# Five edits at the start of a two-block transformer kernel: input squares folded, taps re-spread, one projection from native to split products

## The reference

```python
h = rmsnorm(x, norm_mix_g[0])
u = h @ w_pw1 + b_pw1                 # conformer_conv, 1024 -> 2048
a, gate = split(u); u = a * sigmoid(gate)
u = conv1d_depthwise(u, 31 taps) + b_dw
u = silu(layernorm(u, ln_g, ln_b))
x = x + u @ w_pw2 + b_pw2
h = rmsnorm(x, norm_mem_g[l]); mem_n = rmsnorm(mem, norm_memsrc_g[l])
k = mem_n @ w_k; v = mem_n @ w_v      # for layer l = 0 and l = 1
...                                   # attention, feed forward, the second block
```

## Time and profile before

| | us |
|---|---|
| runs, median (lowest to highest) | 1439.92 (1438.95 to 1442.92) |
| span of the profiled execution | 1437.8 |
| TensorE busy | 1411.5 (98%) |
| VectorE busy | 1111.5 (77%) |
| ScalarE busy | 690.4 (48%) |

### The profile page before, as it was taken

One profiled execution on the slowest core, in us unless ns is written; L12 is line 12 of the kernel. 1 busy time (PEld: TensorE's weight loads), 2 busy tenths in 40 slices (PEclk: granted clock), 3 DMA queues, 4 the chain that ended last, 5 costly groups with the idle time before them and its releaser, 6 DMA issues.

```text
span 1437.8 us, 21872 instructions
## 1 busy us (share of the span) xinstructions
PE 1411.5 (98%) x8580; PEld 1243.6 (86%) x8580; DVE 1111.5 (77%) x1660; ACT 690.4 (48%) x899; POOL 33.1 (2%) x21
## 2 busy tenths in 40 slices
PE   7999999999999999999999999999999999999997
PEld 6878998888889888888888988888988889888887
DVE  3799876698767887758887779997578678798664
ACT  2221664455434654645563355553454447555442
POOL 0000000000000000000000000000024100000000
PEclk9999999999999999999999999999999999999999
DMA  7444663355686456525558747757553436475451
GB/s 265 144 167 153 251 214 123 118 186 208 236 292 207 169 188 219 183 94 182 191 204 279 268 179 273 272 188 260 203 204 135 169 103 226 159 273 205 135 179 66
DMA packets 60150, 279.31 MB, mean 194 GB/s; under 512 B 6590, under 2 KB 8063, under 8 KB 35232
## 3 DMA queue, kind: packets, MB, share of 16 engines
q1 hardware_dynamic: 56248, 270.69, 53.7%
q10 hardware_dynamic: 3816, 7.45, 1.5%
HBM read 273.89 MB, written 4.19 MB: 193 GB/s over the span
## 4 chain that ended last, share of the span: by engine, by line
PE 84%; DVE 8%; DMA 5%; ACT 1%; issue 1%; DVEq 0%; SPq 0%; ACTq 0%
PE acc L477 34%; PE acc L479 17%; PE acc L498 10%; DMA ada_w<-in_ada 5%; PE acc L536 3%; PE acc L538 3%; PE acc L537 3%; DVE wsplit L1753 2%; PE acc L636 2%; PE stat L721 2%; DVE ada_w L2142 2%; PE acc L640 1%; PE turned L741 1%; PE stat L833 1%; PE score L1054 1%
## 5 line engine op out<-in xcount | busy, mean ns | idle before, releaser
L477 PE MATMUL acc<-hA,wsplit 128*128 128x512 f32 x1664 | 589.9, 399 | 4.4 <-DVE tsum L1767 1.7
L1176 ACT ACTIVATE wsplit<-raw 128x2048 fp32r<-128x2048 f32 (+3 forms) x214 | 381.2, 1783 | 195.3 <-PE acc L479 145.1
L1753 DVE TENSOR_TENSOR wsplit<-raw,wsplit 128x2048 fp32r<-128x2048 f32 (+3 forms) x214 | 455.1, 2130 | 16.4 <-ACT wsplit L1176 16.4
L479 PE MATMUL acc<-hA,wsplit 128*128 128x256 f32 x1664 | 463.9, 279 | 0.0
L477 PEld LDWEIGHTS acc<-hA,wsplit 128*128 128x128 f32 x1664 | 312.3, 188 | 81.6 <-issue 4.1
L479 PEld LDWEIGHTS acc<-hA,wsplit 128*128 128x128 f32 x1664 | 313.4, 188 | 0.4
L477 PE MATMUL acc<-hid,wsplit 128*128 128x512 f32 x648 | 224.9, 390 | 0.0
L479 PE MATMUL acc<-hid,wsplit 128*128 128x256 f32 x648 | 182.7, 282 | 0.0
L1186 ACT ACTIVATE lowp<-acc 128x512 f32<-128x512 f32 (+1 forms) x118 | 69.0, 585 | 202.8 <-PE acc L479 174.9
L477 PEld LDWEIGHTS acc<-hid,wsplit 128*128 128x128 f32 x648 | 121.6, 188 | 25.6
L479 PEld LDWEIGHTS acc<-hid,wsplit 128*128 128x128 f32 x648 | 122.5, 189 | 0.0
(11 more groups left out here) (315 smaller groups left out, 2051.6 us busy)
## 6 DMA issues: line engine op xcount, KB each, us to landing
raw<-in_gu SPq DMA_DIRECT2D x44, 1024.0 KB, 4.9
ada_w<-in_ada SPq DMA_DIRECT2D x144, 256.0 KB, 4.8
raw<-in_up SPq DMA_DIRECT2D x32, 1024.0 KB, 4.9
raw<-in_down SPq DMA_DIRECT2D x32, 1024.0 KB, 5.0
raw<-in_dn SPq DMA_DIRECT2D x32, 704.0 KB, 4.1
raw<-in_pw SPq DMA_DIRECT2D x12, 1024.0 KB, 8.1
raw<-in_memk SPq DMA_DIRECT2D x8, 1024.0 KB, 4.8
raw<-in_memv SPq DMA_DIRECT2D x8, 1024.0 KB, 5.3
```

The costliest lines, as they stand in the source:

```text
L477: nc.tensor.matmul(dst.rearrange("p (s t) -> p s t", s=2), w, h, start=start, stop=False, skip_group_check=True)
L479: return nc.tensor.matmul(dst[:, 0:T], lo_w, h[:, 0, :], start=False, stop=stop, skip_group_check=True)
L1176: nc.scalar.activation(wsplit[:, slot, 0, 0:elems_of(n)], raw[:, slot, 0:elems_of(n)], ACT.Copy).then_inc(S("w_hi"), 1)
L1753: V.tensor_tensor(wsplit[:, slot, 1, 0:e], raw[:, slot, 0:e], wsplit[:, slot, 0, 0:e].bitcast(F32), ALU.subtract).then_inc(S("w_lo"), 1)
```

## The change

1. **Input squares folded.** ScalarE writes the squares of x's four pairs to four places (`aux`, `tsum`); VectorE adds them with three additions (semaphore input_folded); TensorE needs 2 matmuls for the sum instead of 8, and issues them inside pw1's chunk 0, ahead of its sixth tile (`inside={(0, 5): input_sums}`), so that pw1 is first in its list. The load of `ones` moves behind that of the first weight chunk.
2. **Taps re-spread.** Each `expand` issues 2 taps before its product instead of 11, and then `BESIDE_PW1[c]` taps behind it: 97 in all during pw1 instead of 77.
3. **memk1 becomes a split stage** (`split_keys`, three matmuls for each tile into one bank). ScalarE's four `split_hi` stand in memv0's copies and behind them; VectorE's four `mem_lo` and three of the four `split_lo` come before the last taps.
4. **`ln_mean`** moves from behind memk1's chunk 2 to its tile 3.
5. **VectorE's later splits** all move back by a place: memv1's by one each, pw2's chunk 1 from between two `ln_lo` to behind the last one.

```diff
-NATIVE = ["pw1", "memk0", "memv0", "memk1"]
+NATIVE = ["pw1", "memk0", "memv0"]
+BESIDE_PW1 = [13, 12, 12, 16, 16, 2, 12, 0]
...
+            def split_keys():
+                st = STAGE["memk1"]
+                for c in range(st.chunks):
+                    weights_ready(st, c)
+                    pe.wait_ge(S("memory_kept"), 2 * (KT // 2) + c - 1)
+                    for kt in range(KT):
+                        if c == 0:
+                            pe.wait_ge(S("mem_lo"), kt // 2 + 1)
+                        if (c, kt) == (2, 3):
+                            ln_mean()
+                        for j in range(2):
+                            at = kt * 2 * P + j * P
+                            mm = whole_tile(acc[:, c % 2, j, 0:T], wsplit[:, c, 0, at:at + P], wsplit[:, c, 1, at:at + P],
+                                            tile_of(hA)(kt), kt == 0, kt == KT - 1)
+                    mm.then_inc(S("chunk_done"), 1)
...
-            pe.wait_ge(S("ones_loaded"), 16)
-            norm_sums("mix0")
+            def input_sums():
+                pe.wait_ge(S("ones_loaded"), 16)
+                pe.wait_ge(S("input_folded"), 3)
+                for j in range(2):
+                    mm = nc.tensor.matmul(stat[:, 0, :], ones[:], aux[:, 0, j, :], start=j == 0, stop=j == 1)
+                mm.then_inc(S("norm_stat"), 1)
...
-            native("memk1", mem_h[1], {kt: (S("mem_h"), KT + kt + 1) for kt in range(KT)},
-                   after=lambda c: ln_mean() if c == 2 else None)
+            split_keys()
             split_values()
...
+            nc.scalar.preload_act_table_set("natural_log_exp_and_others")
+            wait("x_loaded", 16)
+            for p in range(PAIRS):
+                nc.scalar.activation((aux if p < 2 else tsum)[:, p % 2, :, :], x[:, 2 * p:2 * p + 2, :],
+                                     ACT.Square).then_inc(S("norm_sq"), 1)
             wait("cols_loaded", 16)
...
+            def keys_ahead(c):
+                if c > 0:
+                    split_hi(STAGE["memk1"], c - 1, c - 1)
+                    return
+                wait("skew_stored", 16 * G_HEADS)
+                for p in range(PAIRS):
+                    wait("mem_h", KT + 2 * p + 2)
+                    nc.scalar.activation(hA[:, 2 * p:2 * p + 2, 0:T], mem_h[1][:, 2 * p:2 * p + 2, :],
+                                         ACT.Copy).then_inc(S("mem_hi"), 1)
+            memory_out("memv0", lambda c: mv0[:, :, c * T:(c + 1) * T], keys_ahead)
+            split_hi(STAGE["memk1"], 3, 3)
...
-                conv_taps(11, c)
+                conv_taps(2, c)
                 wait("pw1_sig", c + 1)
...
+                conv_taps(BESIDE_PW1[c], c + 1)
...
-            conv_taps(KT * TAPS, KT)
+            conv_taps(100, KT)
+            for p in range(PAIRS):
+                wait("mem_hi", p + 1)
+                V.tensor_tensor(hA[:, 2 * p:2 * p + 2, T:2 * T], mem_h[1][:, 2 * p:2 * p + 2, :],
+                                hA[:, 2 * p:2 * p + 2, 0:T].bitcast(F32), ALU.subtract).then_inc(S("mem_lo"), 1)
+            for c in range(3):
+                split_lo(STAGE["memk1"], c, c)
+                conv_taps(13 if c < 2 else KT * TAPS, KT)
...
             ln_fold(0, tsum[:, 0, :, :], tsum[:, 1, :, :], LN_MEAN)
-            for p in range(PAIRS):
-                wait("mem_hi", p + 1)
...
-            split_lo(STAGE["memv1"], 0, 0)
+            split_lo(STAGE["memk1"], 3, 3)
             wait("ln_stat", 1)
...
-            split_lo(STAGE["memv1"], 3, 3)
+            split_lo(STAGE["memv1"], 2, 2)
             ln_product(0)
             ln_product(1)
             ln_lo(0)
-            split_lo(STAGE["pw2"], 0, 0)
+            split_lo(STAGE["memv1"], 3, 3)
             ln_product(2)
             ln_lo(1)
-            split_lo(STAGE["pw2"], 1, 1)
+            split_lo(STAGE["pw2"], 0, 0)
             ln_product(3)
             ln_lo(2)
             ln_lo(3)
-            split_lo(STAGE["pw2"], 2, 2)
-            split_lo(STAGE["pw2"], 3, 3)
+            for c in range(1, STAGE["pw2"].chunks):
+                split_lo(STAGE["pw2"], c, c)
```

More of the change, by code:

```diff
@@ L175, in stat_count @@
 def stat_count(q):
-    return sum(2 if n in FOLDED else PAIRS for n, _ in NORMS[:q])
+    return sum(1 if n == "mix0" else 2 if n in FOLDED else PAIRS for n, _ in NORMS[:q])
 LN_TABLE = 3
+BESIDE_PW1 = [13, 12, 12, 16, 16, 2, 12, 0]
 LN_MEAN, LN_SQUARES = 3, 6
@@ L404, in _ @@
             sp.dma_start(cols[:], dram["cols"]).then_inc(S("cols_loaded"), 16)
-            sp.dma_start(ones[:], dram["ones"]).then_inc(S("ones_loaded"), 16)
             def load(st, c, known):
@@ L418, in _ @@
                 load(PLAN[0], c, c)
-                if c == 1:
+                if c == 0:
+                    sp.dma_start(ones[:], dram["ones"]).then_inc(S("ones_loaded"), 16)
+                elif c == 1:
                     for tensor, name in ((taps, "taps"), (ident, "ident"), (onehot, "onehot"), (relT, "relT"),
@@ L480, in block_cols, with native @@
                                         skip_group_check=True)
-            def native(name, h, ready=None, after=None):
+            def native(name, h, ready=None, after=None, inside={}):
                 st = STAGE[name]
@@ L490, in native @@
                     for kt in range(KT):
+                        if (c, kt) in inside:
+                            inside[c, kt]()
                         if c == 0 and ready and kt in ready:
@@ L873, in behind_pw1 @@
                     norm_sums("mem", [2 * c - 6, 2 * c - 5])
-            native("pw1", pw1_h, {2 * p: (S("pw1_h"), p + 1) for p in range(PAIRS)}, after=behind_pw1)
+            native("pw1", pw1_h, {2 * p: (S("pw1_h"), p + 1) for p in range(PAIRS)}, after=behind_pw1,
+                   inside={(0, 5): input_sums})
             def relative_biases(c):
@@ L1445, in log_sigmoid @@
                 nc.scalar.activation(za_, zl_, ACT.Ln, bias=1.0).then_inc(S(sem + "_ln"), 1)
+            nc.scalar.preload_act_table_set("natural_log_exp_and_others")
[3 more added lines that the diff above has]
+                                     ACT.Square).then_inc(S("norm_sq"), 1)
             wait("cols_loaded", 16)
-            log_table("mix0")
-            norm_squares("mix0", x, lambda p: [("x_loaded", 16)])
+            nc.scalar.activation(rstd[:, 0:1], col("rms_eps"), ACT.Ln).then_inc(S("log_table"), 1)
             norm_root("mix0")
@@ L1555, in _ @@
             beside = {
-                (0, 0): lambda: value_hi(0),
-                (0, 1): lambda: (ln_table(), value_hi(1)),
+                (0, 0): lambda: (ln_table(), value_hi(0)),
+                (0, 1): lambda: value_hi(1),
                 (0, 2): lambda: (ln_squares(range(PAIRS)), value_hi(2)),
@@ L1560, in _ @@
                 (1, 0): lambda: (ln_silu(0), ln_silu(1), ln_hi(0)),
-                (1, 1): lambda: (pw2_hi(0), ln_silu(2), ln_hi(1)),
-                (1, 2): lambda: (pw2_hi(1), ln_silu(3)),
+                (1, 1): lambda: (ln_silu(2), ln_hi(1), pw2_hi(0)),
+                (1, 2): lambda: (ln_silu(3), pw2_hi(1)),
                 (1, 3): lambda: (ln_hi(2), ln_hi(3), pw2_hi(2), pw2_hi(3)),
@@ L1565, in _ @@
             memory_out("memk0", lambda c: mk0[:, 2 * c:2 * c + 2, :], copy_biases)
-            memory_out("memv0", lambda c: mv0[:, :, c * T:(c + 1) * T])
-            wait("skew_stored", 16 * G_HEADS)
-            for p in range(PAIRS):
-                nc.scalar.activation(hA[:, 2 * p:2 * p + 2, 0:T], mem_h[1][:, 2 * p:2 * p + 2, :],
-                                     ACT.Copy).then_inc(S("mem_hi"), 1)
+            def keys_ahead(c):
[9 more added lines that the diff above has]
+            split_hi(STAGE["memk1"], 3, 3)
             memory_out("memk1", spill_at(0), spill_out(0))
@@ L2153, in _ @@
                 last.then_inc(S("pw1_h"), 1)
+            for i, (into, part) in enumerate(((aux[:, 0, :, :], aux[:, 1, :, :]), (tsum[:, 0, :, :], tsum[:, 1, :, :]),
+                                              (aux[:, 0, :, :], tsum[:, 0, :, :]))):
+                wait("norm_sq", 2 * i + 2 if i < 2 else PAIRS)
+                if i == 2:
+                    wait("input_folded", 2)
+                V.tensor_tensor(into, into, part, ALU.add).then_inc(S("input_folded"), 1)
             norm_scale("mix0")
@@ L2218, in _ @@
             ln_fold(0, tsum[:, 0, :, :], tsum[:, 1, :, :], LN_MEAN)
-            for p in range(PAIRS):
-                wait("mem_hi", p + 1)
-                V.tensor_tensor(hA[:, 2 * p:2 * p + 2, T:2 * T], mem_h[1][:, 2 * p:2 * p + 2, :],
-                                hA[:, 2 * p:2 * p + 2, 0:T].bitcast(F32), ALU.subtract).then_inc(S("mem_lo"), 1)
-            split_lo(STAGE["memv1"], 0, 0)
+            split_lo(STAGE["memk1"], 3, 3)
             wait("ln_stat", 1)
@@ L2229, in _ @@
                 V.tensor_tensor(c2, c2, spread(mu[:], 2), ALU.subtract).then_inc(S("ln_centred"), 1)
-            split_lo(STAGE["memv1"], 1, 1)
+            split_lo(STAGE["memv1"], 0, 0)
```

(2 more changed lines are left out.)

## The result

| | before | changed |
|---|---|---|
| runs, median (lowest to highest), us | 1441.1 (1438.95 to 1442.92, 5 runs) | 1448.59 (1446.3 to 1450.01, 5 runs) |
| ratio, 95% interval | | 1.0057 (1.0046 to 1.0067) |
| span of the profiled execution | 1437.8 | 1444.5 |
| TensorE busy | 1411.5 | 1406.8 |

A forecast was written before the change was run, and what follows sets the result against it. TensorE was taken as the bound, gapless before 190 us. Terms -1.6 - 4.5 + 6.2 + 1.5 + 4.0 = +5.6 us on 1439.9 gave 1445.5 us, 0.4% slower, range 1441 to 1449.

The forecast's parts named there:

- The input squares, -1.6: Kernel start: pw1 begins first, its chunk 0 ends at 18.8 instead of 20.4, a gain of 1.6 us.
- my bound of 9.2: Start of pw1: earliest time for its first matmul, if the 0.5 us earlier chunk issue counts fully; 9.5 forecast.
- The taps, 0: During pw1: 20 extra taps use VectorE's idling; worth 0 by itself, 8 us to VectorE later.
- memk1's products, -4.5: memk1 on TensorE: a chunk costs 5.8 instead of 6.93 us; four give a gain of 4.5 us.
- The first wait, 6.2: memk1's chunk 2, tile 3: TensorE waits 6.2 us for VectorE's folds; bounds 5 and 7.
- The remark behind its sum: After the first wait's sum: TensorE's asking date moves forward 5.5 us, with 9.1 us of splits ahead of the folds.
- M + 34.7: TensorE's asking date for the folds before the change, given as 153.2; M, memv0's chunk 1 end, was 118.5.
- M + 27.6: TensorE's new asking date for the folds, at memk1's chunk 2, tile 3; M is memv0's chunk 1 end on TensorE.
- The layer norm behind it, 0: Behind the first wait: squares' folds 9.9 us after the sum, asked for at 12.2; no wait, up to 1 us possible.
- The second wait, 3.9 to 4.0: pw2's chunk 1: TensorE waits 3.9, say 4.0 us, for VectorE's split, now behind ln_lo(2) and ln_lo(3); bounds 0 and 4.5.
- The clock, 1.5 and 0: Half-rate work costs 1.5 us after the first wait, bounds 0 and 3; clock should hold at pw2's second wait.
- The rival with both falls: Both waits, in memk1 and pw2, trip the clock: +7.1 us, 1447.0; chance 9%.

The follow-up runs named there:

- the dummy matmuls at the start: Both waits mended, plus 64 dummy bf16 matmuls while TensorE waits for its first weights: ratio 0.9925, median 1429.16 us.
- the mended kernel: Changed kernel with 112 taps ahead of memk1's first split, last taps given to the tile furthest behind, pw2's second split ahead of ln_lo: ratio 0.9956, median 1434.6 us.
- the filler: Changed kernel with 45 dummy bf16 matmuls ahead of the wait for the folds at memk1's chunk 2: ratio 1.0041, median 1445.63 us.
- the kernel with 112 taps: Changed kernel with 112 instead of 100 taps ahead of memk1's first split, 13 instead of 25 at the end: ratio 1.0017, median 1442.12 us.

## Why the prediction had the two waits right and the clock wrong

- **The input squares, -1.6.** Measured -1.3 in the profile of the changed kernel, -2.2 and -0.3 in the two that hold the squares without memk1's change. The mechanism holds (pw1 begins at 9.3, the sums are ready, the removed 5.3 us aren't won), but I took the half-rate stretch for a fixed 1.5 us. It cost 2.0 in the changed kernel's profile, which a start 0.2 earlier than forecast partly made up, and 1.5 to 3.1 over the eight profiles; and the other seven begin pw1 between 8.70 and 9.13, all ahead of my bound of 9.2. Nor is it true that chunk 0 "cannot avoid" the stretch: the dummy matmuls at the start avoid it. By the ratio those two kernels gain 2.9 and 2.6 us, with intervals from 1.2 to 4.5, so -1.6 lies within them; the runs don't fix the term more closely.
- **The taps, 0.** Right: the kernel with them ties with the one without.
- **memk1's products, -4.5.** Right. It shows where nothing waits: from memv0's last copy to memv1's last the mended kernel takes 47.8 us, before 52.4.
- **The first wait, 6.2.** Measured 6.3. (The remark behind its sum, that TensorE's asking date moves forward by 5.5 us, doesn't follow from the terms: from M + 34.7 to M + 27.6 is 7.1, and the profiles show that. Nothing hangs on it.) Its two causes were right and separable: VectorE idling for the first high part (5.08 us; 12 taps moved into it return 5.0 of the wait) and the taps alone on the last tile (mended: the rest).
- **The layer norm behind it, 0.** Right: no wait in memv1.
- **The second wait, 3.9 to 4.0.** Measured 3.9 in all three executions that have it alone or beside the first; one move on each of two engines removes it.
- **The clock, 1.5 and 0.** This is the step that failed. "Resuming at half rate costs what it did at the start, 1.5" was mis-sized: 2.5, by the profile and by the filler. "The clock should hold (4.0 against 4.3)" was wrong: it fell, and cost 1.8, and 2.9 in the kernel with 112 taps. I took one fall, 4.3 us after the last matmul, for a threshold; with 112 taps it fell 3.0 us after the last matmul. The rival with both falls, to which I gave 9%, is what happened; with 2.5 + 1.8 in place of its 1.5 + 1.5 it gives +8.4, and with the start's -1.3 in place of -1.6 it gives +8.7, the shift of the marks. The Trainium skill, "TensorE: Matmul & The Clock Gate", Part 1, speaks of a throttled default state that sustained activity releases. These traces agree: behind both waits work resumed with the clock at or about to fall to 0.50, and it was 1.00 again only after 5.3 and 4.2 us of work. I should have given that rule more weight at the second wait.

The split products of memk1, then, did what they do on TensorE's list (4.5 us less), and with the moves made for them on the other lists they cost 14.5 us, over three times that (6.3 + 2.5 + 3.9 + 1.8), because VectorE's waits for ScalarE now stood ahead of work that TensorE was about to ask for.

## What to carry to other kernels

When a bound engine gets less to do, its asking dates move forward: recount every supplier's list against the new dates, and put work that waits for nothing ahead of work that waits. Price a stall of the matmul engine at its length plus a stretch at half clock, here 1.8 to 2.9 us after stalls of 3.9 to 6.3 and none after a stall of 1.3 (with 112 taps); a few dummy matmuls in the stall, or at the kernel's start, buy that back. Keep independent chains' last links balanced, so that none runs alone at the end.

## What the runs showed of the hardware

- The half-rate stretch has no fixed length: 6.8 us after the first wait of the changed kernel (1.6 of them still idle), 3.4 after the second, and 6.8 after the same second wait with 112 taps (0.9 idle). Nor does the fall come at one distance from the last matmul: 4.7 us behind it at both waits of the changed kernel, 3.0 with 112 taps, 4.3 at the end of the run of before. It can come after TensorE has resumed: at 194.0, with work since 193.19.
- At a program's start the clock column prints 1.00 while the records are at half rate; the spacing of the records is the one to read.
- Pairs of a 512- and a 256-column fp32r matmul start 0.347 us apart in some stretches and 0.353 in others, and where the slower ones lie differs from execution to execution. Behind 1250 us they are 0.353 apart until about 1360 in the profile of before, but only from about 1289 to 1300 in that of the changed kernel. The rows are starts of a pair's first matmul; in the first two three pairs lie between them (1.06 us), in the last two one:

```profile
1301.19 0.24 PE acc L477
1302.25 0.24 PE acc L477
```

```profile
1304.53 0.23 PE acc L480
1304.87 0.23 PE acc L480
```

This makes up most of the 2.2 us by which the two profiles close up between 1250 and 1414 us; up to 1250 us the shift stays within 0.6 us of what it was at pw2. What sets the spacing I haven't found, and it is open.
